# Key norms and sine products on GpSimd, query norms inside the score pass, in a two-layer hybrid attention kernel

## The chip, the cores and the metric

One core of one Trainium2 chip. The metric is the device time of one launch, in microseconds (us). Three runs of the kernel before gave 1128.81, 1129.51 and 1130.82 us; their median is 1129.51 us.

## The reference, cut to what matters

Two layers, each a SwiGLU block, an attention mixer and a second SwiGLU block, on 256 tokens of width 1024. The mixer has three branches, a (4 query heads, 2 key heads, window 128), b (4 heads through latents) and c (8 query heads, compressed, selected and windowed keys). The change touches these lines of it:

```
def rms_norm(x, g):
    y = xf * lax.rsqrt(jnp.mean(xf * xf, axis=-1, keepdims=True) + EPS)
    return (y * g).astype(x.dtype)
def apply_rope(x, cos, sin):
    return concatenate([x1 * c - x2 * s, x2 * c + x1 * s])

qa = apply_rope(rms_norm(heads(a_q, A_HEADS), a_qk_g[0]), cos64, sin64)
ka = apply_rope(rms_norm(heads(a_k, A_KV_HEADS), a_qk_g[1]), cos64, sin64)
qc = rms_norm(heads(c_q, C_HEADS), c_qk_g[0])
qc_rot = apply_rope(qc, cos64, sin64)
k_cmp = rms_norm(compress_blocks(heads(c_kc, C_KV_HEADS), ...), c_qk_g[1])
s = jnp.einsum('bqhgd,bjhd->bhgqj', qc, k_cmp).astype(jnp.float32) * scale   # then masked softmax over 15 keys
```

A query's norm is one number per token and head, so it can be applied to the query or to the query's row of scores. The scale is 64 ** -0.5 for a and c and 96 ** -0.5 for b.

## The kernel before, in words

There is no planner: the order of the work is written out by hand, one program for each engine, and semaphores tie them. `PREP` names the steps that VectorE (DVE) finishes in the mixer, in order: lat, qb, kb, qa, kc, cq, cr, ck, cmp. `AUX` names small results that TensorE (PE) puts into four PSUM banks in turn (`aux_open` waits until the one four places before has been copied out), with the engine that copies each out. SyncE issues the large weight loads; GpSimd (POOL) builds the rotary tables at the start and is idle after that. `link` marks an instruction whose result the next one on the same engine waits for.

The mixer's weights are projected in five chunks. The last two, F_CQ (c's queries) and F_CK (c's selected and windowed keys and values), are projected in split precision: for each of four quarters q, ScalarE (ACT) rounds the rows into `mwh` (`round_rows`, L1327), DVE forms the remainder `mwl` (`rest_rows`, L1915), and PE multiplies (`project_split`, L861, L862, and L866, which is the part that reads `mwl`). `copy_proj` (L1286, L1287) on ACT squares and copies a finished chunk to SBUF.

DVE's part (`mixer` in the vector program), in its order: norm of a's queries and keys (`heads_rstd`, `by_rstd`), remainders of F_CQ's quarters 0 and 1, rotation of a's heads (step qa), remainders of quarters 2 and 3; then the compressed keys, `kcn`, 15 partitions by 2 heads of 64: square, sum, inverse root in eight small instructions (`rsqrt`, L1488 to L1495), product with the root, with the gain, twice, into `kcd` (step kc); remainders of F_CK's quarters 0 to 2; the norm of c's queries in place (step cq); the remainder of F_CK's quarter 3; the rotation of c's queries (`rope`: one product with the cosines L1537, two halves with the sines L1538 and L1539, one sum L1549; step cr).

PE's part: `project_split(F_CQ)`, turns of qa, ka (`doubled`) and kc, `scores(l, 0)`, `project_split(F_CK)`, then a loop over n from 1: `scores(n)`, for n = 1 the turns of c's normed queries cq0 and cq1, then `values(n - 2)`, `turn_probs(n - 1)`, for n = 1 the compressed scores (L1063), and from n = 4 on the output projection `mix_out` (L723, L725, L727), which first waits for `cmpT`.

The 12 units n are pairs of heads: 0 and 1 of a, 2 and 3 of b, 4 to 11 of c, selected and windowed in turn. For each head, `rescore` on DVE (L1980 for 128 columns, L1982 for 256) reads the scores from PSUM, multiplies them by `-scale`, adds the mask and takes the row's minimum; ACT takes the exponentials (`exponents`); `normalise` on DVE multiplies by the reciprocal of the sum. Between units 1 and 4 DVE also does `key_norms` and `key_ropes` for the selected and windowed keys, `compressed_scores` (L2020 to L2024) and `compressed_probs`:

```
                    V.tensor_tensor_reduce(e[:, 0:P], ps[:, i, 0:P], cst[:, C_CAUSAL:C_CAUSAL + P], -scale, least,
                                           ALU.add, ALU.min, st[:, 2:3])
```

`least` is a per-partition value from memory (`nsink`) for branch a and the number 3e38 for the others; `-scale` is a number for all.

Of the kernel before, what the change touches and what calls it, by code (L numbers as in the profile page):

```python
# [33 lines left out]
I32 = mybir.dt.int32  # L34
ALU = mybir.AluOpType
# [75 lines left out]
def hybrid_kernel(nc, x, c, positions, ada_w, ada_b, norm_g, ffn_w_in, ffn_w_out, w_in, w_out,  # L111
                  a_sinks, a_qk_g, b_q_lat_g, b_kv_lat_g, b_w_uq, b_w_ukv, b_qk_nope_g, b_qk_rope_g,
                  c_qk_g, c_cmp_pe, c_cmp_w1, c_cmp_w2, c_gate_w, c_gate_b, consts, out):
    with ExitStack() as ctx:
        def sb(name, shape, dt=F32):
            return ctx.enter_context(nc.sbuf_tensor(name, shape, dt))

        def sem(name):
            return ctx.enter_context(nc.semaphore(name))
# [117 lines left out]
        def ET(n, i):  # L237
# [6 lines left out]
        csc = fa[:, :, 0:C_H * NCMP].rearrange("p a (h b) -> p a h b", h=C_H)  # L244
        trg = cqT[:, 0:3, :].rearrange("p a n -> p (a n)")
        kwt = sb("kwt", [P, SEQ])
        cst16 = sb("cst16", [P, 3, NT * C_H])


# [132 lines left out]
        def head(n, i):  # L382

            br, hh = UNITS[n][0], 2 * UNITS[n][1] + i
            half = slice(64 * i, 64 * i + 64)
            if br == "a":
                return (qaT[half, hh // 2, :], kaT[half, hh // 2, :],
                        lambda t: pa[:, t, 384 + hh // 2 * HD:384 + hh // 2 * HD + HD], cst[:, C_BAND:C_CAUSAL + P], SC64)
            if br == "b":
                return qbT[:, hh, :], kbT[:, hh, :], lambda t: kvb[:, t, hh, HD:P], mlate[:, :], SC96  # L390
            win = int(br == "win")
            kv = hh // 4
            off = 256 + 128 * win + kv * HD
            return (crT[half, hh // 2, :], ckT[half, 2 * win + kv, :],
                    lambda t: pk[:, t, off:off + HD], mlate[:, :], SC64)

        def head_at(l, n, i):

# [208 lines left out]
        def _(pe):  # L607
# [337 lines left out]
            def mixer(l):  # L945
# [83 lines left out]
                cq = pq[:, :, :].rearrange("p t (a n) -> p t a n", a=C_H)  # L1029

                for n in range(1, NU + 3):
                    if n < NU:
                        if n == 4:
# [1 line left out]
                            pe.wait_ge(*aux_done("kw", l))  # L1035
                        scores(l, n)
                    if n == 1:
                        pe.wait_ge(prep, prep_at(l, "cq"))
                        pairs("cq0", cq, (0, 1))
                        pairs("cq1", cq, (2, 3))  # L1040
# [78 lines left out]
        def _(act):  # L1119
# [177 lines left out]
            def mixer(l):  # L1297
# [54 lines left out]
                for q in range(3):  # L1352
# [5 lines left out]
                nc.scalar.copy(kcT[:, :, 0:NCMP], ps[:, aux_bank("kc"), 0:2 * P].rearrange("p (g b) -> p g b", g=2)  # L1358
                               [:, :, 0:NCMP]).then_inc(aux_act, 1)

                round_rows(F_CK, 3)

                def exponents(n, i):
# [19 lines left out]
                    exponents(0, i)  # L1383
                copy_proj(l, 4)
                for n in range(1, NU + 1):
                    if n == 1:
                        out_of(l, "cq0", cqT[:, 0:2, :])
                        out_of(l, "cq1", cqT[:, 2:4, :])
                    if n == 2:
                        out_of(l, "cr0", crT[:, 0:2, :])  # L1390
                        out_of(l, "cr1", crT[:, 2:4, :])
                    for i in range(2):
                        if n < 3 and i == 0:
                            turned_probs(n - 1, 0)
# [27 lines left out]
        def _(pool):  # L1422
# [46 lines left out]
                i = V.tensor_copy(cs[:, 1, :, hf:2 * hf], tv[:, 1, :, lo:lo + hf])  # L1469
            i.then_inc(tables, 1)  # L1470


        @block.vector
        def _(dve):
# [7 lines left out]
                ins.then_inc(chain_s, 1)  # L1482
                dve.wait_ge(chain_s, chain["n"])

            def rsqrt(n, p=P):

                s, t, r = ssb[0:p, 0:n], newt[0:p, 0:n], rst[0:p, 0:n]
                link(ts(r.bitcast(I32), s.bitcast(I32), -0.5, float(0x5F3759DF), ALU.mult, ALU.add))  # L1488
                link(tt(t, r, r, ALU.mult))
                link(stt(t, t, -0.1875, s, ALU.mult, ALU.mult))  # L1490
                link(stt(r, t, 0.5625, r, ALU.add, ALU.mult))
                link(tt(t, r, r, ALU.mult))
                link(stt(t, t, 64.0 / 9.0, s, ALU.mult, ALU.mult))
                link(stt(t, t, 10.0 / 3.0, t, ALU.subtract, ALU.mult))
                link(stt(r, t, 5.0, r, ALU.add, ALU.mult))  # L1495

            def heads_rstd(src, dim, tmp=None):

                p, a, n, d = src.shape
                if tmp is None:  # L1500
# [328 lines left out]
            def mixer(l):  # L1829
# [121 lines left out]
                spread = lambda ap, n=C_H: ap.rearrange("p (t b) -> p t b", t=NT).unsqueeze(2)\  # L1951
# [19 lines left out]
                def rescore(n, i):  # L1971
# [44 lines left out]
                def compressed_scores():  # L2016
# [94 lines left out]
```

## Time and profile before

| | us |
|---|---|
| median of the runs | 1129.51 |
| the profiled execution, its own time | 1130.08 |
| its span, first to last instruction | 1128.3 |
| PE busy | 1084.1 (96%) |
| DVE busy | 831.3 (74%) |
| ACT busy | 499.5 (44%) |
| POOL busy | 12.0 (1%), all before 22.2 us |

The mixers stand at 220 to 380 us (layer 0) and 766 to 926 us (layer 1) of the span. The numbers below are of layer 0; layer 1 repeats them 546.2 us later. "us" in a row is a time from the start of the span, then a duration. In a timeline "[2.72 <-ACT mwh L1327]" means that the engine had been idle for 2.72 us, and what ended it. The granted clock of TensorE is given as a share of its full speed.

### The profile page before, as it was taken

What the parts mean: (1) busy time and instruction counts of PE and PEld (TensorE: products, weight loads), DVE (VectorE), ACT (ScalarE), POOL (GpSimd) and SP (SyncE); (2) the same over time, 40 slices, a digit from 0 to 9 for tenths busy, and PEclk for the clock granted to TensorE, in tenths of its full rate; (3) what the DMA queues carried; (4) which work ended last, traced back from release to release, by engine and by line L of the source; (5) the groups of instructions that cost most, each with busy time, mean ns of one, the idle gap of its engine ahead of it and who ended that gap; (6) DMA issues with size and microseconds to landing.
All of it is one profiled execution on the core that took longest, in us unless ns stands there. A gap on an engine that the chain in (4) does not pass through costs nothing.

```text
span 1128.3 us, 13797 instructions
## 1 busy us (share of the span) xinstructions
PE 1084.1 (96%) x5221; PEld 837.4 (74%) x5221; DVE 831.3 (74%) x1502; ACT 499.5 (44%) x868; POOL 12.0 (1%) x30
## 2 busy tenths in 40 slices
PE   5999999999989999999999999999998999999998
PEld 1688888865766588888878888886576667888887
DVE  1766997886988785876687789886879787655644
ACT  2543342324567563343534433422255566433431
POOL 4000000000000000000000000000000000000000
PEclk9999999999989999999999999999998999999999
DMA  9799999454612179896439999954582113876631
GB/s 360 259 378 363 372 378 326 148 180 129 224 62 76 38 252 330 305 325 209 162 113 334 342 387 384 355 194 156 115 294 80 53 61 115 269 250 230 199 112 74
DMA packets 149366, 253.70 MB, mean 225 GB/s; under 512 B 9639, under 2 KB 119861, under 8 KB 141109
## 3 DMA queue, kind: packets, MB, share of 16 engines
q1 hardware_dynamic: 148596, 251.53, 65.1%
q10 hardware_dynamic: 704, 1.30, 0.3%
q8 instruction: 41, 0.67, 0.2%
q14 instruction: 25, 0.20, 0.1%
HBM read 251.76 MB, written 1.05 MB: 224 GB/s over the span
## 4 chain that ended last, share of the span: by engine, by line
PE 84%; DVE 11%; ACT 2%; issue 1%; DMA 1%; SPq 0%; DVEq 0%; ACTq 0%
PE ps L693 12%; PE ps L695 12%; PE ps L694 12%; PE ps L723 8%; PE ps L727 8%; PE ps L725 8%; PE ps L845 6%; DVE mwl L1915 2%; PE ps L705 2%; PE ps L674 1%; PE ps L672 1%; PE ps L673 1%; PE ps L901 1%; DMA wide<-in_ada_w_dram 1%; PE ps L890 1%
## 5 line engine op out<-in xcount | busy, mean ns | idle before, releaser
L693 PE MATMUL ps<-wh,uh 128*128 128x512 f32 x576 | 227.2, 395 | 0.0
L695 PE MATMUL ps<-wlo,uh 128*128 128x512 f32 x576 | 224.5, 390 | 0.0
L694 PE MATMUL ps<-wh,ul 128*128 128x512 f32 x576 | 224.3, 389 | 0.0
L1645 DVE TENSOR_TENSOR wlo<-wide,wh 128x1024 fp32r<-128x1024 f32 x176 | 207.6, 1220 | 15.7 <-ACT wh L1183 13.9
L1183 ACT CAST wh<-wide 128x1024 fp32r<-128x1024 f32 x176 | 175.9, 1049 | 16.7 <-DMA wide<-in_ffn_w_in_dram 16.7
L1255 ACT ACTIVATE fs<-ps 128x512 f32<-128x512 f32 x40 | 24.0, 599 | 282.3 <-PE ps L695 273.1
L1800 DVE TENSOR_TENSOR fa<-fs,ps 128x512 f32<-128x512 f32 x40 | 27.5, 688 | 137.8 <-ACT fs L1255 137.2
L723 PE MATMUL ps<-th,fh 128*128 128x512 f32 x320 | 128.1, 400 | 0.0
L695 PEld LDWEIGHTS ps<-wlo,uh 128*128 128x128 f32 x576 | 108.1, 188 | 23.0
L727 PE MATMUL ps<-tlo,fh 128*128 128x512 f32 x320 | 125.0, 390 | 0.0
L725 PE MATMUL ps<-th,fl 128*128 128x512 f32 x320 | 124.6, 390 | 0.0
L694 PEld LDWEIGHTS ps<-wh,ul 128*128 128x128 f32 x576 | 108.3, 188 | 21.6
L693 PEld LDWEIGHTS ps<-wh,uh 128*128 128x128 f32 x576 | 108.2, 188 | 21.4
L1673 DVE TENSOR_TENSOR tlo<-tall,th 128x1024 fp32r<-128x1024 f32 x104 | 123.4, 1219 | 0.0
L1656 DVE SCALAR_TENSOR_TENSOR acc<-ada,cond,acc 128x2048 f32<-128x2048 f32 (+1 forms) x49 | 100.2, 2044 | 22.9 <-DMA ada<-in_ada_w_dram 22.5
L1190 ACT CAST th<-tall 128x1024 fp32r<-128x1024 f32 x104 | 105.2, 1051 | 10.8 <-DMA tall<-in_ffn_w_out_dram 10.8
L725 PEld LDWEIGHTS ps<-th,fl 128*128 128x128 f32 x320 | 60.2, 188 | 12.7 <-issue 1.0
L727 PEld LDWEIGHTS ps<-tlo,fh 128*128 128x128 f32 x320 | 60.0, 188 | 12.8
L723 PEld LDWEIGHTS ps<-th,fh 128*128 128x128 f32 x320 | 60.1, 188 | 12.6 <-issue 1.0
L845 PE MATMUL ps<-wide,u 128*128 128x416 f32 (+2 forms) x192 | 68.6, 515 | 0.3
L845 PEld LDWEIGHTS ps<-wide,u 128*128 128x128 f32 x192 | 36.0, 190 | 29.5 <-issue 23.6
L1195 ACT CAST fh<-ps 128x512 fp32r<-128x512 f32 x40 | 23.5, 587 | 60.3 <-PE ps L705 60.3
(363 smaller groups left out, 1548.2 us busy)
## 6 DMA issues: line engine op xcount, KB each, us to landing
wide<-in_ffn_w_in_dram SPq DMA_DIRECT2D x176, 512.0 KB, 6.6
ada<-in_ada_w_dram SPq DMA_DIRECT2D x60, 1024.0 KB, 7.1
tall<-in_ffn_w_out_dram SPq DMA_DIRECT2D x44, 1024.0 KB, 5.2
wide<-in_w_in_dram SPq DMA_DIRECT2D x14, 1024.0 KB, 7.5
tall<-in_w_out_dram SPq DMA_DIRECT2D x8, 1024.0 KB, 8.6
ada<-in_ada_w_dram SPq DMA_DIRECT2D x16, 512.0 KB, 5.9
wide<-in_c_cmp_w_dram SPq DMA_DIRECT2D x4, 1024.0 KB, 10.1
wide<-in_w_in_dram SPq DMA_DIRECT2D x4, 832.0 KB, 7.9
```

What stands on the lines that cost most here:

```text
L693: mm(o, uh[:, k, rows_], wh[:, hsl, :, k, :], start=(k == 0), stop=False, skip_group_check=True)
L694: mm(o, ul[:, k, rows_], wh[:, hsl, :, k, :], start=False, stop=False, skip_group_check=True)
L695: i = mm(o, uh[:, k, rows_], wlo[:, s, :, k, :], start=False, stop=(k == KD - 1), skip_group_check=True)
L723: mm(y[:, t, hf, :], hi[:, toks], th[:, slot, a, cols], start=(first and x == 0), stop=False, skip_group_check=True)
L725: mm(y[:, t, hf, :], lo[:, toks], th[:, slot, a, cols], start=False, stop=False, skip_group_check=True)
L727: i = mm(y[:, t, hf, :], hi[:, toks], tlo[:, slot, a, cols], start=False, stop=(last and x == len(rows) - 1), skip_group_check=True)
L845: i = mm(ps[:, banks + t, 0:width], u[:, k, t * P:(t + 1) * P], wv[:, k, :], start=(k == 0), stop=(k == KD - 1))
L1183: nc.scalar.copy(wh[:, (n + 1) % 2, :, 2 * c:2 * c + 2, :], raw).then_inc(wh_ready, 1)
L1190: nc.scalar.copy(th[:, n % 2, m % 2, :], tall[:, n % 2, m % 2 * DM:(m % 2 + 1) * DM]).then_inc(th_ready, 1)
L1645: tt(wlo[:, n % 2, :, ks, :], raw, wh[:, (n + 1) % 2, :, ks, :].bitcast(F32), ALU.subtract)\
L1656: stt(part, piece, cond[:, k:k + 1], part, ALU.mult, ALU.add).then_inc(ada_used, 1)
L1673: tt(tlo[:, n % 2, m % 2, :], tall[:, n % 2, m % 2 * DM:(m % 2 + 1) * DM], th[:, n % 2, m % 2, :].bitcast(F32), ALU.subtract).then_inc(tl_ ...
```

## The change

- GpSimd gets `key_norm(l)`: it waits for the copy-out of "w2" (ACT) and for step lat, then norms the compressed keys with 23 instructions: 17 products or sums of two tensors and 6 with constants, each linked to the next except the first of the last two. It increments `kc_normed`, for which PE's turn of kc now waits. DVE's block for it goes; steps kc and cq go from `PREP`.
- GpSimd gets `sine_halves(l)`: after the copy of c's query projection and step qa, the two sine products of c's rotation into `T2` (512 elements per partition each). DVE does the cosine product, waits for `sines`, and adds.
- c's queries are no longer multiplied by their root (L1945). `score_root` puts the negated root, with the 1/8 of the scale in it, into `qroot`, and for branch a into `aroot`; `rescore` takes its multiplier from there, a column of memory per token block, in place of the number. Branch b keeps a number. Of a's six heads DVE now multiplies only the two key heads by their root, and a's key table has a factor -8.
- The compressed scores are multiplied by the roots in one added DVE instruction of 240 elements; the maximum becomes a minimum, and the exponential's scale -1. Their buffer `csc` moves from `fa` to `ada`.
- PE's turns of cq0 and cq1, now of unnormed queries, move from n = 1 to between the turn of kc and `scores(l, 0)`, behind a wait for the copy of the projection; ACT's copies of them move before its rounding of F_CK's quarter 3.
- The rotary tables with gain (`gained`) are made by an instruction with a constant factor in place of a plain product.

```diff
-        PREP = ["lat", "qb", "kb", "qa", "kc", "cq", "cr", "ck", "cmp"]
+        PREP = ["lat", "qb", "kb", "qa", "cr", "ck", "cmp"]
...
-                pe.wait_ge(prep, prep_at(l, "kc"))
+                pe.wait_ge(kc_normed, l + 1)
                 turn(l, "kc", [(P * g, kcd[:, g, :, :].rearrange("p a n -> p (a n)")) for g in range(2)])
+                pe.wait_ge(pcopy, l * 10 + 8)
+                cq = pq[:, :, :].rearrange("p t (a n) -> p t a n", a=C_H)
+                pairs("cq0", cq, (0, 1))
+                pairs("cq1", cq, (2, 3))
                 pe.wait_ge(*aux_done("ka", l))
                 pe.wait_ge(pcopy, l * 10 + 6)
                 scores(l, 0)
...
+                out_of(l, "cq0", cqT[:, 0:2, :])
+                out_of(l, "cq1", cqT[:, 2:4, :])
                 round_rows(F_CK, 3)
...
+            def key_norm(l):
+                pool.wait_ge(*aux_done("w2", l))
+                pool.wait_ge(prep, prep_at(l, "lat"))
+                kc, tmp = kcn[0:NCMP, :, :], kcd[0:NCMP, :, 0, :]
+                s, t, r = (cst16[0:NCMP, x, 0:2] for x in range(3))
+                link(tt(tmp, kc, kc, ALU.mult))
+                w = HD // 2
+                while w > 1:
+                    link(tt(tmp[:, :, 0:w], tmp[:, :, 0:w], tmp[:, :, w:2 * w], ALU.add))
+                    w //= 2
...
+            def sine_halves(l):
+                pool.wait_ge(pcopy, l * 2 * len(CHUNKS) + 2 * 4)
+                pool.wait_ge(prep, prep_at(l, "qa"))
+                tt(t2[:, :, :, 0:hf], cq[:, :, :, hf:HD], wide_(cs[:, :, 0:hf]), ALU.mult)
+                tt(t2[:, :, :, hf:HD], cq[:, :, :, 0:hf], wide_(cs[:, :, hf:HD]), ALU.mult).then_inc(sines, 1)
...
-                dve.wait_ge(*aux_done("w2", l))
-                kc = kcn[0:NCMP, :, :].unsqueeze(2)
-                heads_rstd(kc, HD)
-                by_rstd(kc, kc)
-                for dup in range(2):
-                    i = gain(kc, G_C + HD, kcd[0:NCMP, :, dup, :].unsqueeze(2))
-                i.then_inc(prep, 1)
-                dve.wait_ge(prep, prep_at(l, "kc"))
...
-                heads_rstd(cq, HD, v4(cq2[:, :, :], C_H))
-                r = rst[:, 0:NT * C_H].rearrange("p (a n) -> p a n", a=NT).unsqueeze(3).broadcast_to([P, NT, C_H, HD])
-                tt(cq, cq, r, ALU.mult).then_inc(prep, 1)
-                dve.wait_ge(prep, prep_at(l, "cq"))
+                roots = score_root(qroot, v4(cq2[:, :, :], C_H))
                 rest_rows(F_CK, 3)
-                rope(cq, cs_of(T_CQ), [qr[:, :, :, :]]).then_inc(prep, 1)
+                t1, t2 = (ap[:, :].rearrange("p (a n d) -> p a n d", a=NT, n=C_H) for ap in (T1, T2))
+                link(tt(t1, cq, cs_of(T_CQ)[:, 0, :, :].unsqueeze(2).broadcast_to([P, NT, C_H, HD]), ALU.mult))
+                dve.wait_ge(sines, l + 1)
+                tt(qr[:, :, :, :], t1, t2, ALU.add).then_inc(prep, 1)
...
-                    V.tensor_tensor_reduce(e[:, 0:P], ps[:, i, 0:P], cst[:, C_CAUSAL:C_CAUSAL + P], -scale, least,
+                    V.tensor_tensor_reduce(e[:, 0:P], ps[:, i, 0:P], cst[:, C_CAUSAL:C_CAUSAL + P], scale[0], least,
...
-                    link(V.tensor_reduce(over(0), csc, AX.X, ALU.max))
+                    link(tt(csc, csc, roots.unsqueeze(3).broadcast_to([P, NT, C_H, NCMP]), ALU.mult))
+                    link(V.tensor_reduce(over(0), csc, AX.X, ALU.min))
```

## Rows read from the trace of the kernel before

**Rows 1.** Timeline of DVE, layer 0's mixer: start, duration, engine, line, operation, forms, [idle].
```profile
281.49 2.36 DVE L1915 TENSOR_TENSOR mwl<-wide,mwh 128x1024 fp32r<-128x1024 f32 x2 [2.72 <-ACT mwh L1327]
...
287.54 2.36 DVE L1915 TENSOR_TENSOR mwl<-wide,mwh 128x1024 fp32r<-128x1024 f32 x2
...
292.42 0.48 DVE L1516 TENSOR_TENSOR kcd<-kcn,gn 15x128 f32<-15x128 f32 x2
...
296.35 1.21 DVE L1503 TENSOR_REDUCE ssb<-cq 128x16 f32<-128x1024 f32 x1
...
299.48 1.23 DVE L1945 TENSOR_TENSOR acc<-acc,rst 128x1024 f32<-128x1024 f32 x1
...
303.02 0.69 DVE L1538 TENSOR_TENSOR sq<-acc,fa 128x512 f32<-128x512 f32 x1
...
305.81 0.35 DVE L1980 CUSTOM_DVE_ANT_0 acc<-ps,cst,nsink 128x128 f32<-128x128 f32 x1
...
309.74 0.34 DVE L1980 CUSTOM_DVE_ANT_0 early<-ps,cst,nsink 128x128 f32<-128x128 f32 x1
...
318.99 0.29 DVE L1980 CUSTOM_DVE_ANT_0 acc<-ps,cst 128x128 f32<-128x128 f32 x1
...
321.05 0.41 DVE L2024 TENSOR_TENSOR fa<-fa,cst 128x240 f32<-128x240 f32 x1
```

**Rows 2.** Timeline of PE, the same mixer.
```profile
288.91 1.10 PE L866 MATMUL ps<-mwl,muh 128*128 128x512 f32 x4
...
293.46 0.38 PE L878 MATMUL ps<-cst,kcd 128*128 128x128 f32 x2
295.41 0.93 PE L890 MATMUL ps<-kaT,qaT 64*128 64x128 f32 x8 [1.57 <-ACT kaT L1295]
296.27 0.50 PE L861 MATMUL ps<-mwh,muh 128*128 128x512 f32 x1
...
307.38 0.93 PE L890 MATMUL ps<-kaT,qaT 64*128 64x128 f32 x8
...
332.25 0.47 PE L723 MATMUL ps<-th,uh 128*128 128x512 f32 x1 [2.20 <-ACT cmpT L1295]
```

**Rows 3.** Timeline of ACT, the same mixer.
```profile
282.36 0.25 ACT L1349 COPY vrep<-ps 128x128 f32<-128x128 f32 x1
...
293.78 0.60 ACT L1287 COPY acc<-ps 128x512 f32<-128x512 f32 x1
...
309.75 0.57 ACT L1279 COPY acc<-ps 128x512 f32<-128x512 f32 x1
...
364.98 0.40 ACT L1370 ACTIVATE sq<-sq,stat 128x128 f32<-128x128 f32 x1 [0.70 <-DVE stat L1982]
```

**Rows 4.** Windows: stretch, then length and busy (count) per engine, PEclk, DMA share, GB/s.
```profile
330.00:340.00 10.00, 7.80 (x39) 5.84 (x39) 6.62 (x31) 5.42 (x18) 0.00 (x0) 0.83 0.00 0
340.00:350.00 10.00, 10.00 (x65) 6.95 (x65) 7.84 (x35) 6.88 (x22) 0.00 (x0) 1.00 0.33 106
```

**Rows 5.** Timeline of POOL at the start of the kernel.
```profile
8.70 0.35 POOL L1447 TENSOR_TENSOR cqT<-cst,posf 128x96 f32<-128x96 f32 x1
...
13.79 0.59 POOL L1456 TENSOR_TENSOR cqT<-cqT 128x192 f32<-128x192 f32 x1
14.47 0.69 POOL L1455 TENSOR_SCALAR cqT<-cqT 128x192 f32<-128x192 f32 x1
```

**Rows 6.** Timeline of DVE at the start of the kernel.
```profile
12.27 0.16 DVE L1583 SCALAR_TENSOR_TENSOR rst<-newt,rst 128x1 f32<-128x1 f32 x1
...
13.92 0.48 DVE L1583 SCALAR_TENSOR_TENSOR rst<-newt,rst 128x1 f32<-128x1 f32 x1
...
14.74 0.16 DVE L1585 SCALAR_TENSOR_TENSOR newt<-newt 128x1 f32<-128x1 f32 x1
```

**Rows 7.** Chain of work that ended last, two steps of the output projection.
```profile
333.25 0.43 PE ps L723
...
339.99 0.23 PE ps L723
```

More of the change, by code:

```diff
@@ L243, in hybrid_kernel @@
         cp = fs[:, :, :].rearrange("p a (h b) -> p a h b", h=C_H)
-        csc = fa[:, :, 0:C_H * NCMP].rearrange("p a (h b) -> p a h b", h=C_H)
+        csc = ada[:, 0, 0:NT * C_H * NCMP].rearrange("p (a h b) -> p a h b", a=NT, h=C_H)
         trg = cqT[:, 0:3, :].rearrange("p a n -> p (a n)")
         kwt = sb("kwt", [P, SEQ])
+        aroot, qroot = sb("aroot", [P, NT * 6]), sb("qroot", [P, NT * C_H])
         cst16 = sb("cst16", [P, 3, NT * C_H])
@@ L282, in hybrid_kernel @@
         chain_s = sem("chain")
+        kc_normed, sines = sem("kc_normed"), sem("sines")
         muh_ready, mul_ready_, mwh_ready, mwl_ready, mwh_used = (
@@ L387, in head @@
                 return (qaT[half, hh // 2, :], kaT[half, hh // 2, :],
-                        lambda t: pa[:, t, 384 + hh // 2 * HD:384 + hh // 2 * HD + HD], cst[:, C_BAND:C_CAUSAL + P], SC64)
+                        lambda t: pa[:, t, 384 + hh // 2 * HD:384 + hh // 2 * HD + HD], cst[:, C_BAND:C_CAUSAL + P],
+                        [aroot[:, 6 * t + hh:6 * t + hh + 1] for t in range(NT)])
             if br == "b":
-                return qbT[:, hh, :], kbT[:, hh, :], lambda t: kvb[:, t, hh, HD:P], mlate[:, :], SC96
+                return qbT[:, hh, :], kbT[:, hh, :], lambda t: kvb[:, t, hh, HD:P], mlate[:, :], [-SC96, -SC96]
             win = int(br == "win")
@@ L394, in head @@
             return (crT[half, hh // 2, :], ckT[half, 2 * win + kv, :],
-                    lambda t: pk[:, t, off:off + HD], mlate[:, :], SC64)
+                    lambda t: pk[:, t, off:off + HD], mlate[:, :],
+                    [qroot[:, C_H * t + hh:C_H * t + hh + 1] for t in range(NT)])
         def head_at(l, n, i):
@@ L1037, in mixer @@
                     if n == 1:
-                        pe.wait_ge(prep, prep_at(l, "cq"))
-                        pairs("cq0", cq, (0, 1))
-                        pairs("cq1", cq, (2, 3))
                         pe.wait_ge(pcopy, l * 10 + 10)
@@ L1385, in mixer @@
                 for n in range(1, NU + 1):
-                    if n == 1:
-                        out_of(l, "cq0", cqT[:, 0:2, :])
-                        out_of(l, "cq1", cqT[:, 2:4, :])
                     if n == 2:
@@ L1400, in mixer @@
                             act.wait_ge(cmp_shift, l + 1)
-                            A(csc, csc, ACT.Exp, scale=SC64).then_inc(cmp_exp, 1)
+                            A(csc, csc, ACT.Exp, scale=-1.0).then_inc(cmp_exp, 1)
                         if n == 4 and i == 0:
@@ L1470, in _ @@
             i.then_inc(tables, 1)
+            def key_norm(l):
[8 more added lines that the diff above has]
+                    w //= 2
+                link(tt(s.unsqueeze(2), tmp[:, :, 0:1], tmp[:, :, 1:2], ALU.add))
+                link(ts(s, s, 1.0 / HD, EPS, ALU.mult, ALU.add))
+                link(ts(r.bitcast(I32), s.bitcast(I32), -0.5, float(0x5F3759DF), ALU.mult, ALU.add))
+                v = cst16[0:NCMP, 2, 2:4]
+                link(tt(t, r, r, ALU.mult))
+                link(tt(t, t, s, ALU.mult))
+                link(ts(t, t, -0.1875, 0.5625, ALU.mult, ALU.add))
+                link(tt(r, t, r, ALU.mult))
+                link(tt(t, r, r, ALU.mult))
+                link(tt(t, t, s, ALU.mult))
+                link(ts(t, t, 64.0 / 9.0, None, ALU.mult))
+                link(ts(v, t, -10.0 / 3.0, None, ALU.add))
+                link(tt(t, t, v, ALU.mult))
+                link(ts(t, t, 5.0, None, ALU.add))
+                link(tt(r, t, r, ALU.mult))
+                link(tt(kc, kc, r.unsqueeze(2).broadcast_to([NCMP, 2, HD]), ALU.mult))
+                g = gn[0:NCMP, G_C + HD:G_C + 2 * HD].unsqueeze(1).broadcast_to([NCMP, 2, HD])
+                for dup in range(2):
+                    i = tt(kcd[0:NCMP, :, dup, :], kc, g, ALU.mult)
+                i.then_inc(kc_normed, 1)
+                pool.wait_ge(kc_normed, l + 1)
@@ new lines, in sine_halves @@
+            def sine_halves(l):
+                hf, cs = HD // 2, fa[:, 0, :].rearrange("p (e t n) -> p e t n", e=2, t=NT)[:, 1, :, :]
+                cq = pq.rearrange("p t (n d) -> p t n d", n=C_H)
+                t2 = T2.rearrange("p (a n d) -> p a n d", a=NT, n=C_H)
+                wide_ = lambda ap: ap.unsqueeze(2).broadcast_to([P, NT, C_H, hf])
+                pool.wait_ge(pcopy, l * 2 * len(CHUNKS) + 2 * 4)
+                pool.wait_ge(prep, prep_at(l, "qa"))
+                tt(t2[:, :, :, 0:hf], cq[:, :, :, hf:HD], wide_(cs[:, :, 0:hf]), ALU.mult)
+                tt(t2[:, :, :, hf:HD], cq[:, :, :, 0:hf], wide_(cs[:, :, hf:HD]), ALU.mult).then_inc(sines, 1)
@@ L1473, in _ @@
+            for l in range(DEPTH):
+                key_norm(l)
+                sine_halves(l)
         @block.vector
@@ L1483, in link, with rsqrt @@
                 dve.wait_ge(chain_s, chain["n"])
-            def rsqrt(n, p=P):
-                s, t, r = ssb[0:p, 0:n], newt[0:p, 0:n], rst[0:p, 0:n]
-                link(ts(r.bitcast(I32), s.bitcast(I32), -0.5, float(0x5F3759DF), ALU.mult, ALU.add))
+            def rsqrt(n, p=P, root=None):
+                s, t, r = ssb[0:p, 0:n], newt[0:p, 0:n], rst[0:p, 0:n] if root is None else root
+                seed = float(0x5F3759DF) if root is None else float(0x5F3759DF - 2 ** 31)
+                link(ts(r.bitcast(I32), s.bitcast(I32), -0.5, seed, ALU.mult, ALU.add))
                 link(tt(t, r, r, ALU.mult))
@@ L1505, in heads_rstd, with score_root @@
                 rsqrt(a * n, p)
+            def score_root(root, sums):
+                p, a, n, d = sums.shape
+                link(V.tensor_reduce(ssb[:, 0:a * n].rearrange("p (a n) -> p a n", a=a), sums, AX.X, ALU.add))
+                link(ts(ssb[:, 0:a * n], ssb[:, 0:a * n], HD * EPS, None, ALU.add))
+                rsqrt(a * n, root=root[:, :])
+                return root[:, :].rearrange("p (a n) -> p a n", a=a)
             def by_rstd(src, dst):
@@ L1524, in gained @@
             def gained(lo, a):
-                hf, c = HD // 2, cs_of(a)
+                hf, c, by = HD // 2, cs_of(a), -8.0 if a == T_AK else 1.0
                 g = lambda x, y: gn[:, lo + x:lo + y].unsqueeze(1).broadcast_to([P, NT, y - x])
-                tt(c[:, 0, :, :], cs64[:, 0, :, :], g(0, HD), ALU.mult)
-                tt(c[:, 1, :, 0:hf], cs64[:, 1, :, 0:hf], g(hf, HD), ALU.mult)
-                return tt(c[:, 1, :, hf:HD], cs64[:, 1, :, hf:HD], g(0, hf), ALU.mult)
+                stt(c[:, 0, :, :], cs64[:, 0, :, :], by, g(0, HD), ALU.mult, ALU.mult)
+                stt(c[:, 1, :, 0:hf], cs64[:, 1, :, 0:hf], by, g(hf, HD), ALU.mult, ALU.mult)
+                return stt(c[:, 1, :, hf:HD], cs64[:, 1, :, hf:HD], by, g(0, hf), ALU.mult, ALU.mult)
             def turned_halves(src, cs, t1, t2):
@@ L1919, in mixer @@
                 qk = v4(pa[:, :, 0:384], 6)
-                heads_rstd(qk, HD, v4(qk2[:, :, :], 6))
-                by_rstd(qk, qk)
+                root = score_root(aroot, v4(qk2[:, :, :], 6))[:, :, A_H:6].unsqueeze(3).broadcast_to([P, NT, A_KV, HD])
+                link(tt(qk[:, :, A_H:6, :], qk[:, :, A_H:6, :], root, ALU.mult))
                 for q in range(2):
@@ L1979, in rescore @@
                         dve.wait_ge(pt_ready, head_at(l, n - 2, i))
-                    V.tensor_tensor_reduce(e[:, 0:P], ps[:, i, 0:P], cst[:, C_CAUSAL:C_CAUSAL + P], -scale, least,
+                    V.tensor_tensor_reduce(e[:, 0:P], ps[:, i, 0:P], cst[:, C_CAUSAL:C_CAUSAL + P], scale[0], least,
                                            ALU.add, ALU.min, st[:, 2:3])
-                    V.tensor_tensor_reduce(e[:, P:3 * P], ps[:, i, P:3 * P], head(n, i)[3], -scale, least,
+                    V.tensor_tensor_reduce(e[:, P:3 * P], ps[:, i, P:3 * P], head(n, i)[3], scale[1], least,
                                            ALU.add, ALU.min, st[:, 3:4]).then_inc(nm_ready, 1)
```

1 line of the change is left out of this document (removed).

## The prediction, made before the change was run

> **What bounds the kernel now.** I read the timelines of DVE, PE and ACT over layer 0's mixer side by side, then the windows; layer 1 repeats them. Three stretches matter.
>
> First, 281.5 to 307.4 us: PE multiplies F_CQ and F_CK almost without a gap. Quarter 2's part that reads `mwl` starts at 288.91 [rows 2], and DVE's pair of remainders for quarters 2 and 3 runs from 287.54 for 2.36 us [rows 1], so quarter 2's is ready at about 288.7: PE has 0.2 us to spare there. The turn of kc starts at 293.46; then PE is idle 1.57 us until ACT has copied `kaT`, does `scores(0)` at 295.41, starts F_CK at 296.27 and `scores(1)` at 307.38 [rows 2].
>
> Second, 306 to 332 us: DVE is the bound. Its scan of unit 1 starts at 309.74 [rows 1], although `scores(1)` began at 307.38 and takes 0.93 us [rows 2], so the scores were there at 308.3. DVE is 1.44 us late, and from there it works without a pause up to the scan of unit 4. PE waits for the result of that, 2.20 us, until `cmpT` at 332.25 [rows 2].
>
> Third, 336 to 380 us: PE is the bound, busy 10.00 of 10 us with DVE at 7.84 [rows 4].
>
> So work taken from DVE before 309.74 is worth 1.44 us per mixer and no more, for behind DVE stands PE's projection of F_CK, which the change does not shorten. Work added to DVE after 309.74 counts in full until 332. Work added on PE's way before 307.4 counts where it exceeds those 1.44 us.
>
> **Part by part (us, per mixer).**
>
> *Key norm off DVE.* DVE's block lies between the remainders' end (287.54 + 2.36 = 289.90) and 292.42 + 0.48 = 292.90 [rows 1]: 3.0 go. The remainders of F_CK then end at about 293.5, and DVE waits for the copy of the projection, 293.78 + 0.60 = 294.38 [rows 3], where the reduction for the roots can start instead of at 296.35 [rows 1]: 2.0 are left.
>
> *Query product and sine halves off DVE.* The product is 1.23, the halves two of 0.69 which overlap to 1.2 [rows 1]. DVE would be ready for the first scan at 305.81 - 2.0 - 1.2 - 1.2 = 301.4. All that counts of these 4.4 is the 1.44, as unit 1's scan must wait for PE.
>
> *A's query product* falls away where DVE idles 2.72 us for `mwh` [rows 1]: nothing. That idle time hides it; were it gone, 0.7 would count. *Tables with gain*: an operation of the same size, under PE's earlier projections; nothing, between -0.3 and +0.3.
>
> *Root column as the multiplier.* The scan of 128 columns takes 0.35 and 0.34 with one operand from memory (`nsink`) and 0.29 with none [rows 1]: 0.06 per instruction. I take it to add up for the second column of branch a. Unit 1 has four such instructions, +0.24; the first head of unit 4, on which the end of the DVE stretch hangs, two, +0.12. The other units of c have 0.24 each under PE. At the end of the mixer ACT waits for such a scan (0.70 at 364.98 [rows 3]); that may cost between 0 and 0.2, I take 0.
>
> *Roots on the compressed scores.* One more instruction of 240 elements: 0.41 [rows 1] and a link, +0.44, in full.
>
> *Turns of cq0 and cq1.* They go into PE's gap before 295.41: the projection's copy ends at 294.38, eight turns take about 0.9 (half of the 0.38 that two take, as they overlap), and `kaT` is there at 295.4. I take 0, between 0 and +0.3. They leave n = 1, which is under DVE; nothing. ACT's two copies before F_CK's quarter 3 have 8 us until PE needs it.
>
> *Key norm on GpSimd.* It can start at 282.61 (end of ACT's L1349 [rows 3]). A product of 96 elements takes 0.35 there and one of 192 takes 0.59 [rows 5], that is 0.11 + 0.0025 per element; one with a constant on 192 takes 0.69 [rows 5], some 0.2 on two elements; from 0.59 at 13.79 to the next start at 14.47 a link costs 0.09. Seventeen products: four of 128 elements at 0.43, one each of 64, 32, 16, 8 and 4 at 0.27, 0.19, 0.15, 0.13 and 0.12, eight of two at 0.12; with six of 0.21 and the links 6.9 in all, done at 289.5. PE wants the result at 293.46. Undisturbed, the move has 4 us of cover.
>
> *The same beside DVE.* What the trace shows of two-tensor work on both engines at once: DVE's L1583 takes 0.16 at 12.27, and 0.48 at 13.92, where GpSimd's product ran from 13.79 to 14.38; it ended at 14.40, with it [rows 6, 5]. L1585 at 14.74, inside GpSimd's constant product (14.47 to 15.16), took its 0.16 [rows 6, 5]. So GpSimd's two-tensor products hold up DVE's two-tensor instructions, its constant ones don't. The opposite direction has no row, and from 282.6 to 293.5 DVE does nothing but two-tensor instructions: remainders of 1.18 and the rotation.
>
> The Trainium skill ("SBUF — State Buffer", section "Who interferes with whom") says that a VectorE instruction with two SBUF inputs and a GpSimd instruction that reads SBUF exclude each other, and that whichever comes second is held until the first has ended. The row at 13.92 agrees with it; the row at 14.74 does not, since there GpSimd read SBUF with one input and VectorE was not held. By that rule in both directions the sum would be the +5.4 below, and without it the -1.3.
>
> Bounds: (a) nothing is held: 0. (b) DVE alone is held. Between its remainders of quarters 1 and 2 stand nine rotation instructions, and GpSimd's first seven products fall among them: 0.43 + 0.27 + 0.19 + 0.15 + 0.13 + 0.12 + 0.12 = 1.41. Quarter 2's remainder comes at 290.1, PE wanted it at 288.91: PE is 1.2 late from there. (c) Both are held, in turn. Then GpSimd gets one product per DVE instruction; one more passes in the rotation and nine are left. Five pass with the five remainders, 5 x 1.3, until 295.4; the last four, three of them of 128 elements, need 2.1: done at 297.5. PE, at the turn of kc at 294.7, waits 2.8. Behind that wait stand the turns of kc, cq0, cq1 and `scores(0)` (0.4 + 0.9 + 0.9), then F_CK: it starts at 299.6 instead of 296.27, +3.3.
>
> *Sine products.* 512 elements at 0.0025 + 0.11 are 1.4 each, from 294.4 to 297.2, and DVE wants them at 300. Holding DVE's small steps costs 1.5 of the 6 us that it has until 308.3. Nothing.
>
> **The sum.** With DVE out of the way, the stretch after `scores(1)` starts 1.44 early and has 0.24 + 0.44 + 0.12 = 0.80 more work. Per mixer: (a) -1.44 + 0.80 = -0.64; (b) -0.64 + 1.2 = +0.6; (c) -0.64 + 3.3 = +2.7. For two mixers -1.3, +1.1 and +5.4. The row at 13.92 speaks for (b) at least; whether a DVE instruction holds GpSimd is open, but a resource that one of two engines waits for is likely one that both wait for. I take the middle of (b) and (c), +3.3: the profiled execution's 1130.08 becomes 1133.4, and the median, 0.57 under it, 1129.51 + 3.3 = 1132.8.
>
> **Rivals.**
> 1. *No interference.* GpSimd is done by 290, PE never waits, -1.3: 1128.2. For it: the key norm occupies 15 partitions only, its products are short, and L1583 is a single row. Against it: that row's end, to 0.02 us. This is the case on the other side; it decides as soon as `kc_normed` comes before 294 and quarter 2's remainder before 288.9.
> 2. *The slow stretch of PE goes too.* After its 2.20 us of waiting, PE runs at a granted clock of 0.83 in the mean of 330 to 340 [rows 4]: steps of 0.43 where the same take 0.23 at full clock (2.4 GHz against the lower level's 1.2) [rows 7]; twelve of them stand in that state, 2.4 us. If in case (a) another spacing keeps the clock up in both mixers: 1128.2 - 4.8 = 1123.4; in one, 1125.8. Against it: the wait before it, for DVE, stays as long.
> 3. *The scans become the bound after 336.* Eight units of c at 0.24 are 1.9 per mixer. All of it on the path on top of (a): -1.3 + 3.8 = +2.5, 1132.0. Against it: DVE has 2.2 of 10 us free [rows 4].
> 4. *The sines come late.* GpSimd starts them only after the key norm. In case (c) that is 297.5, done at 300.3, still before 308.3 + 3.3. Only at double the price would it count: +1 per mixer over (c).
>
> **How the numbers follow.** Interference 0.50, rival 1 0.27, rival 2 0.11, rival 3 0.07, rival 4 or something else that is late 0.05. A change of 0.2% (2.3 us) is what can be told from none here. Interference puts 0.40 above that and 0.10 within; rival 1 0.20 within and 0.07 below, by a part of rival 2's gain; rival 2 below; rival 3 above; the last 0.03 above, 0.02 within. So faster 0.18, same 0.32, slower 0.50. The forecast's own range is 1130.6 to 1135.0; the range over cases 1127.0 to 1136.0, which leaves out rival 2 and the far end of rival 4.
>
> **What would show it.** Interference: GpSimd's first products at several times 0.43 and 0.27, ending with DVE's remainders; DVE's rotation longer than before by 1.4; a wait of PE at quarter 2 and at the turn of kc. Right without it: key norm done in 7 us. In either case scans at 0.35 in c, a start of unit 1's scan 0.9 after `scores(1)`, a DVE stretch 0.8 longer up to `cmpT`. The prediction is wrong if PE starts F_CK within 0.5 of its old distance from 281.5.

## The result: 7.8 us slower

The changed kernel took 1137.49 us (median of 4 runs, 1136.35 to 1139.64) against 1129.71 us for the kernel before (median of 4, the extra run included): 1.0070 times the time, 95% interval 1.0057 to 1.0082. The direction was the forecast's, the size more than twice its 3.3 us, and above the upper end of its own range, 1135.0, and of the range over cases, 1136.0.

The profiled execution took 1136.35 us, its span 1134.5. From the page of the changed kernel, busy time by engine:

```profile
span 1134.5 us, 13819 instructions
...
PE 1086.5 (96%) x5221; PEld 837.6 (74%) x5221; DVE 831.8 (73%) x1470; ACT 500.4 (44%) x868; POOL 42.0 (4%) x80
```

DVE is as busy as before (831.3) although it has 32 instructions fewer: what it gave away it pays back in instructions that are longer. GpSimd's busy time rose by 30 us.

Timeline of GpSimd in layer 0's mixer, after:

```profile
281.91 1.41 POOL L1480 TENSOR_TENSOR kcd<-kcn 15x128 f32<-15x128 f32 x1 [260.11 <-ACT vrep L1352]
283.40 2.57 POOL L1483 TENSOR_TENSOR kcd<-kcd 15x64 f32<-15x64 f32 x5
...
287.24 1.18 POOL L1489 TENSOR_TENSOR cst<-cst 15x2 f32<-15x2 f32 x1
288.50 1.06 POOL L1490 TENSOR_TENSOR cst<-cst 15x2 f32<-15x2 f32 x1
289.65 1.04 POOL L1491 TENSOR_SCALAR cst<-cst 15x2 f32<-15x2 f32 x1
290.77 1.05 POOL L1492 TENSOR_TENSOR cst<-cst 15x2 f32<-15x2 f32 x1
291.91 1.06 POOL L1493 TENSOR_TENSOR cst<-cst 15x2 f32<-15x2 f32 x1
293.05 0.18 POOL L1494 TENSOR_TENSOR cst<-cst 15x2 f32<-15x2 f32 x1
...
294.49 0.18 POOL L1499 TENSOR_TENSOR cst<-cst 15x2 f32<-15x2 f32 x1
...
295.22 0.86 POOL L1503 TENSOR_TENSOR kcd<-kcn,gn 15x128 f32<-15x128 f32 x2
296.15 1.30 POOL L1515 TENSOR_TENSOR sq<-acc,fa 128x512 f32<-128x512 f32 x1
297.42 1.26 POOL L1516 TENSOR_TENSOR sq<-acc,fa 128x512 f32<-128x512 f32 x1
```

Five instructions on two elements take 1.04 to 1.18 us; the sixth, of the same size, takes 0.18. DVE over the same time:

```profile
282.99 0.89 DVE L1596 TENSOR_TENSOR sq<-acc,fs 128x512 f32<-128x512 f32 x1
...
287.15 5.77 DVE L1974 TENSOR_TENSOR mwl<-wide,mwh 128x1024 fp32r<-128x1024 f32 x5
294.04 1.22 DVE L1561 TENSOR_REDUCE ssb<-cq 128x16 f32<-128x1024 f32 x1 [1.12 <-ACT acc L1290]
295.29 0.40 DVE L1562 TENSOR_SCALAR ssb<-ssb 128x16 f32<-128x16 f32 x1
295.73 0.38 DVE L1539 TENSOR_SCALAR qroot<-ssb 128x16 int32<-128x16 int32 x1
...
296.35 1.14 DVE L1541 SCALAR_TENSOR_TENSOR newt<-newt,ssb 128x16 f32<-128x16 f32 x1
297.52 1.20 DVE L1542 SCALAR_TENSOR_TENSOR qroot<-newt,qroot 128x16 f32<-128x16 f32 x1
298.75 0.17 DVE L1543 TENSOR_TENSOR newt<-qroot 128x16 f32<-128x16 f32 x1
```

DVE's five remainders run from 287.15 to 292.92, 1.15 apiece, as fast as before [rows 1]. One small GpSimd instruction falls to each; when DVE stops at 292.9 they cost 0.18 again, and still do beside DVE's reduction (294.49, inside L1561). When the small ones are DVE's (L1541, L1542, 0.17 each with the sine products back on DVE, run e2 below) and the long ones GpSimd's sine products, DVE waits. DVE's one-input instructions L1562 and L1539 are not free of it either: 0.40 and 0.38 beside GpSimd's L1503, 0.17 each in the kernel before.

PE in the same mixer (compare [rows 2]), and the windows around its restart:

```profile
288.43 1.19 PE L870 MATMUL ps<-mwl,muh 128*128 128x512 f32 x4
...
296.13 0.44 PE L882 MATMUL ps<-cst,kcd 128*128 128x128 f32 x2 [2.88 <-POOL kcd L1503]
296.40 1.09 PE L882 MATMUL ps<-cst,acc 128*128 128x128 f32 x8
297.42 1.65 PE L894 MATMUL ps<-kaT,qaT 64*128 64x128 f32 x8
299.00 0.79 PE L865 MATMUL ps<-mwh,muh 128*128 128x512 f32 x1
...
310.87 0.93 PE L894 MATMUL ps<-kaT,qaT 64*128 64x128 f32 x8
...
335.13 0.76 PE L727 MATMUL ps<-th,uh 128*128 128x512 f32 x1 [2.32 <-ACT cmpT L1298]
```

```profile
293.00:297.00 4.00, 1.12 (x11) 0.88 (x10) 2.82 (x5) 2.17 (x6) 3.29 (x10) 1.00 0.85 272
297.00:301.00 4.00, 4.00 (x18) 2.77 (x16) 3.79 (x8) 3.54 (x5) 1.68 (x2) 0.57 0.76 252
301.00:305.00 4.00, 4.00 (x19) 3.30 (x18) 3.90 (x10) 0.64 (x4) 0.00 (x0) 1.00 0.00 0
```

I count from DVE's first remainder of F_CQ, 281.49 before [rows 1] and, in the changed kernel's timeline, 280.71 after. F_CK starts at 14.8 before and 18.3 after (+3.5). That is not all waiting: `scores(0)` runs at the lower clock level, 1.65 us instead of 0.93 [rows 2], so some 0.7 of the 3.5 is the clock's. `scores(1)` comes at 25.9 and 30.2 (+4.3, the extra 0.8 is again the clock, granted at 0.57 from 297 to 301); unit 1's scan at 28.3 and 31.1 (+2.9); the output projection at 50.8 and 54.4 (+3.7). The mixer as a whole, from PE's first matmul of F_CQ to the first residual sum, takes 102.7 us in both layers instead of 99.1, two times 3.6 or 7.2 us. The medians differ by 7.8; the spans of the two profiled executions differ by 6.2 (1134.5 and 1128.3), so outside the mixers this one execution was 1.0 shorter than the one before.

Scans with a column from memory, first one of unit 0 and one of unit 1:

```profile
303.44 0.41 DVE L2030 CUSTOM_DVE_ANT_0 acc<-ps,cst,nsink 128x128 f32<-128x128 f32 x1
...
311.83 0.41 DVE L2030 CUSTOM_DVE_ANT_0 early<-ps,cst,nsink 128x128 f32<-128x128 f32 x1 [4.25 <-PE ps L894]
```

### The profile page after: what moved, and what is told of

Its sections match the earlier page's. It is cut to its first block, busy times and chain, and to the rows that moved or that the text cites. A ratio compares the mean times of both kernels' runs of the same rounds, so it can differ in the third digit from the quotient of the medians.

```text
span 1134.5 us, 13819 instructions
## 1 busy us (share of the span) xinstructions
PE 1086.5 (96%) x5221; PEld 837.6 (74%) x5221; DVE 831.8 (73%) x1470; ACT 500.4 (44%) x868; POOL 42.0 (4%) x80
## 3 DMA queue, kind: packets, MB, share of 16 engines
HBM read 251.76 MB, written 1.05 MB: 223 GB/s over the span
## 4 chain that ended last, share of the span: by engine, by line
PE 84%; DVE 7%; POOL 2%; ACT 2%; DMA 2%; issue 2%; SPq 0%; DVEq 0%; POOLq 0%; ACTq 0%
PE ps L699 12%; PE ps L697 12%; PE ps L698 12%; PE ps L727 8%; PE ps L731 7%; PE ps L729 7%; PE ps L849 6%; DMA ada<-in_ada_w_dram 2%; PE ps L709 2%; PE ps L894 1%; PE ps L678 1%; PE ps L676 1%; PE ps L677 1%; PE ps L905 1%; PE ps L663 1%
```

## The experiments

All were timed in five rounds against the kernel before, whose median was 1129.89 in the first four, 1129.47 in the next four and 1129.56 in the last. Each is the changed kernel with an edit, but for e6 and e11. The ratios are not the quotients of the medians; where the two differ by much, as in e6, both are read. "The mixer" is the stretch defined above, in the run's profiled execution.

**e1, the key norm on DVE.**

```diff
-                key_norm(l)            # GpSimd
...
+                dve.wait_ge(*aux_done("w2", l))
+                kc = kcn[0:NCMP, :, :].unsqueeze(2)
+                heads_rstd(kc, HD)
+                by_rstd(kc, kc)
...
+                i.then_inc(kc_normed, 1)
```

> The changed kernel with the compressed keys' norm given back to DVE, at its old place; GpSimd keeps the sine products, everything else of the change stays. Theory (GpSimd's key norm holds up PE's turn of kc): the 2.9 us wait of PE before the turn of kc goes, PE starts F_CK some 14.8 us after F_CQ instead of 18.3, and the time falls by about 4.3 us per mixer, to 1128.0 to 1129.5. Rival A (the root columns and the added product on the compressed scores cost more than thought): still 3 us or more over the kernel before, 1132 or more. Rival B (the sine products are the cause): stays near 1137.

1129.99 us, ratio 0.9997 (0.9989 to 1.0006), 0.5 above the expected range. The whole loss is gone. In its profiled execution each mixer takes 98.7 us, unit 1's scan comes 26.9 after PE's first matmul of F_CQ (28.2 before) and the output projection 23.28 after that scan (22.51 before). Rivals A and B fall.

**e2, the sine products on DVE.**

```diff
-                sine_halves(l)         # GpSimd
...
+                rope(cq, cs_of(T_CQ), [qr[:, :, :, :]]).then_inc(prep, 1)
```

> The changed kernel with the two sine products given back to DVE; GpSimd keeps the key norm. Theory: PE's wait for the key norm stays at 2.9 us, DVE is ready for unit 0 some 1 us later but still waits for PE before unit 1: within 1 us of the changed kernel, 1136.5 to 1138.5. Rival B (the sine products hold DVE's inverse root up, 1.14 and 1.20 us for two instructions, and that is the loss): 3 us or more below the changed kernel.

1138.05 us, ratio 1.0071 (1.0059 to 1.0083), that of the changed kernel (1.0070). L1541 and L1542 of the changed kernel take 0.17 each here instead of 1.14 and 1.20, and PE's wait is 2.85: the 2 us for which the inverse root was held up lie under PE's work.

**e3, PE asks later.** The turn of kc stands behind `scores(1)`.

```diff
-                pe.wait_ge(kc_normed, l + 1)
-                turn(l, "kc", ...)
                 pe.wait_ge(pcopy, l * 10 + 8)
...
                     if n == 1:
+                        pe.wait_ge(kc_normed, l + 1)
+                        turn(l, "kc", ...)
                         pe.wait_ge(pcopy, l * 10 + 10)
```

> The changed kernel, but PE turns kc, and ACT copies it, only after scores(1) and before the compressed scores; cq0 and cq1 come before it. GpSimd does the same work as in the changed kernel. Theory: the key norm is done at about 296 us, PE asks for it at 308, no wait is left, DVE's first remainders are still held a few tenths: 4 us per mixer less than the changed kernel, 1128.0 to 1130.0. Rival C (what GpSimd does to DVE costs by itself, wait or not): 1132 or more. Rival A as before: 1132 or more.

1130.25 us, ratio 1.0009 (0.9999 to 1.0020), 0.25 above the expected range. GpSimd's chain takes as long as in the changed kernel (14.2 us), and nobody waits for it: the loss is PE's wait, and not, in the main, what GpSimd does to DVE. That has a small price: in the profile F_CK still starts 0.4 us later than before, and unit 1's scan comes 27.2 after PE's first matmul of F_CQ where e1 has 26.9. Rivals A and C fall. The twelve runs lie wide, 1127.84 to 1136.46 us, and the profiled one was the slowest: its mixers take 101.5 us, with a granted clock of 0.68 and 0.66 over 320 to 330 and 330 to 340 us where e1 has 1.00 and 0.83. Whether its faster runs had these stretches at full clock, no trace shows.

**e4, a number as the multiplier** (the query norms are left out of the scores of a and c).

```diff
-                        [aroot[:, 6 * t + hh:6 * t + hh + 1] for t in range(NT)])
+                        [-SC64, -SC64])
```

> The changed kernel with the fixed scale in place of the root columns in the score pass of branches a and c; this leaves the query norms out of those scores. Theory: 0.06 us less for each scan with a column, 0.36 us per mixer of them on the path (unit 1 and the first head of unit 4), at most 0.2 more at the end: 0.7 to 1.2 us below the changed kernel, 1136.3 to 1136.8. Rival A: the scans are the bound in the units of c, 2 us per mixer: 1133.5 or less. GpSimd's instructions and PE's wait are the same in both.

1136.45 us, ratio 1.0059 (1.0046 to 1.0072); by the ratios 0.11% or 1.2 us below the changed kernel, though the two intervals overlap. In the profiled execution the mixers take 102.4, 0.35 less each, as forecast for the columns on the path (0.36). The columns are not the bound under PE.

**e5, DVE idle while GpSimd works.**

```diff
+                dve.wait_ge(kc_normed, l + 1)
                 for q in range(3):
                     rest_rows(F_CK, q)
```

> The changed kernel with one wait added on DVE: it begins F_CK's remainders of quarters 0 to 2 only when GpSimd's key norm is done. Theory (each small GpSimd instruction from 287 us on took 1.05 us because a DVE remainder of 1.15 us ran and held it): with DVE idle after quarter 3 of F_CQ, at about 289.4, the rest of the key norm goes at 0.2 us apiece, is done 2.5 to 3 us earlier, PE's wait before the turn of kc falls from 2.9 to under 0.7 us, and the time to 1129.5 to 1131.5. Rival D (these are GpSimd's own prices in a linked chain): the chain is as long as before, PE's wait 2.9 us, the time 1137 or more.

1134.26 us, ratio 1.0043 (1.0026 to 1.0060): a miss, 2.8 us above the expected range. On whether GpSimd's instructions are held, the rows decide. Timelines of e5, GpSimd and then DVE and PE:

```profile
289.06 1.06 POOL L1490 TENSOR_TENSOR cst<-cst 15x2 f32<-15x2 f32 x1
290.21 0.18 POOL L1491 TENSOR_SCALAR cst<-cst 15x2 f32<-15x2 f32 x1
290.47 0.18 POOL L1492 TENSOR_TENSOR cst<-cst 15x2 f32<-15x2 f32 x1
290.74 0.18 POOL L1493 TENSOR_TENSOR cst<-cst 15x2 f32<-15x2 f32 x1
...
294.68 1.75 POOL L1515 TENSOR_TENSOR sq<-acc,fa 128x512 f32<-128x512 f32 x1 [0.64 <-POOL kcd L1503]
296.39 2.27 POOL L1516 TENSOR_TENSOR sq<-acc,fa 128x512 f32<-128x512 f32 x1
```

```profile
294.07 5.67 DVE L1974 TENSOR_TENSOR mwl<-wide,mwh 128x1024 fp32r<-128x1024 f32 x3 [4.00 <-POOL kcd L1503]
299.67 1.21 DVE L1561 TENSOR_REDUCE ssb<-cq 128x16 f32<-128x1024 f32 x1
```

```profile
294.10 0.44 PE L882 MATMUL ps<-cst,kcd 128*128 128x128 f32 x2 [0.31 <-POOL kcd L1503]
```

The same three instructions (L1491 to L1493) that took 1.04 to 1.06 take 0.18 with DVE idle, and PE's wait falls from 2.88 to 0.31. Rival D falls. What the expectation missed: DVE's three remainders start only at 294.07, fall among the sine products and take 5.67; in the kernel before they fit between 292.9 and the reduction at 296.35 [rows 1]. So DVE is late for unit 0, and PE waits 0.67 for its scan before `scores(1)`. In layer 1 the three take 4.57 and PE has no such wait; the mixers take 102.2 and 100.1.

**e6, the sine products alone**, in the kernel before, after step cq.

```diff
+                pool.wait_ge(prep, prep_at(l, "cq"))
+                tt(t2[:, :, :, 0:hf], ...)      # and the other half
...
-                rope(cq, cs_of(T_CQ), [qr[:, :, :, :]]).then_inc(prep, 1)
+                link(tt(t1, cq, ..., ALU.mult))
+                dve.wait_ge(sines, l + 1)
+                tt(qr[:, :, :, :], t1, t2, ALU.add).then_inc(prep, 1)
```

> The kernel before with one part of the change: the two sine products of c's rotation on GpSimd, here after the query norm (step cq), so beside DVE's remainder of F_CK's quarter 3 and its cosine product. Theory of mutual holding: the four two-tensor instructions of the two engines go one after the other, 1.2 + 1.3 + 1.2 + 1.3, then the sum; DVE is ready for unit 0 1.0 to 1.5 us later than before, 1131.5 to 1133. Naive sum (DVE loses 1.2 us): 1127 to 1128.

1133.08 us in the median of 12, ratio 1.0021 (1.0009 to 1.0033). The median is 3.6 us over the kernel before, the ratio says 2.4; the runs spread from 1128.31 to 1134.27, so the size is uncertain, but it is no gain. Timelines of e6, GpSimd, DVE and PE:

```profile
301.29 2.33 POOL L1480 TENSOR_TENSOR sq<-acc,fa 128x512 f32<-128x512 f32 x1 [279.46 <-DVE acc L1959]
303.57 2.29 POOL L1481 TENSOR_TENSOR sq<-acc,fa 128x512 f32<-128x512 f32 x1
```

```profile
301.23 1.23 DVE L1929 TENSOR_TENSOR mwl<-wide,mwh 128x1024 fp32r<-128x1024 f32 x1
302.38 2.32 DVE L1963 TENSOR_TENSOR sq<-acc,fa 128x1024 f32<-128x1024 f32 x1
305.96 1.23 DVE L1965 TENSOR_TENSOR qr<-sq 128x1024 f32<-128x1024 f32 x1 [1.26 <-POOL sq L1481]
```

```profile
308.92 0.93 PE L891 MATMUL ps<-kaT,qaT 64*128 64x128 f32 x8 [0.99 <-DVE stat L1999]
```

Remainder, first half, cosine product, second half: one after the other from 301.2 to 305.9, 4.7 us until the sum. DVE alone needs 3.6 for the same, 300.74 to 304.35 in the kernel before, as a half costs it 0.6 and GpSimd over 1.1. So the move makes DVE 1.1 us later, its scan of unit 0 is late, and PE waits 0.99 for it before `scores(1)`.

**e7, PE kept busy during its wait.**

```diff
+                pe.wait_ge(pcopy, l * 10 + 6)
+                keep_warm(12)
                 pe.wait_ge(kc_normed, l + 1)
```

> The changed kernel with 12 idle multiplications of 512 columns (2.7 us at full clock) on PE in front of its wait for kc_normed. Theory (0.7 us of the loss per mixer is PE at the lower clock level just after the wait, in scores(0) and the first five matmuls of F_CK): the wait's place is filled, F_CK runs at full clock from its start, 0.5 to 0.9 us per mixer less, 1135.5 to 1136.5. If the clock is no part of it: within 0.5 us of 1137.5.

1135.04 us, ratio 1.0048 (1.0036 to 1.0060): 2.4 us under the changed kernel, a little more than expected. `kcd` comes as late, but `scores(0)` takes 0.93 again, F_CK's matmuls follow each other at 0.23 from the second on, and each mixer takes 101.4 us. F_CK starts 17.5 after PE's first matmul of F_CQ (+2.7 over the kernel before instead of +3.5) and `scores(1)` at 28.6 (+2.8 instead of +4.3). So 1.2 to 1.5 us per mixer of the loss is the lower clock level after the wait.

**e8, the gates' arithmetic before unit 1**, with e1's edit, and branch a's queries normed as before.

```diff
+                dve.wait_ge(gate_exp, l + 1)
+                link(ts(gt[:, :, :], gt[:, :, :], 1.0, None, ALU.add))
+                link(V.reciprocal(gt[:, :, :], gt[:, :, :]))
```

> The changed kernel with the key norm on DVE again, and two more edits that take work out of DVE's stretch after unit 1's scan: the gates' sum and reciprocal (0.65 us) done right after c's rotation, where DVE waits for PE, and branch a's queries normed as in the kernel before, with a number as the multiplier (0.24 us at unit 1). Theory (DVE is idle before unit 1 and the bound from there to cmpT): per mixer 0.9 us less than the version with the keys on DVE, 1127.6 to 1128.6, under the kernel before. If that stretch were not DVE's: as that version, 1129.5 to 1130.5.

1128.26 us, ratio 0.9986 (0.9977 to 0.9994): as expected, and 0.14% faster than the kernel before.

**e9, e8 without any GpSimd work in the mixer** (the diffs of e2 and e8 together).

> The version with the gates early (e8), and the sine products back on DVE too: nothing of the mixer is left on GpSimd. In e8 unit 1's scan came 27.5 us after the start of F_CQ, 0.6 later than PE allows, with DVE as the bound. Theory: the sine products add 1.2 us to DVE there and give back 1.0 us of what they held in F_CK's remainders (4.57 us for three in e8, 3.50 before); DVE is the bound, 0 to 0.8 us per mixer more than e8: 1128.3 to 1129.8. If the sine products on GpSimd were worth their full 1.2 us per mixer: 1130.5 or more.

1128.10 us, ratio 0.9982 (0.9972 to 0.9991): as e8, and 0.2 under the expected range. The sine products on GpSimd are worth nothing that can be measured.

**e10, e11, e12: PE kept busy before the output projection**, in e8, in the kernel before and in e9.

```diff
+                    if n == 4:
+                        keep_warm(10, 4)
                     for k in range(KD):
                         if n in MIX_AT[k]:
```

> e8 with 10 idle multiplications of 512 columns on PE in its wait of 2.3 us for cmpT, before the output projection. Theory (the forecast's rival 2: after that wait PE runs a dozen matmuls at the lower clock level, 0.43 us a step where 0.23 is the price at full clock): the slow stretch goes or is halved, 1.0 to 2.4 us per mixer less: 1123.5 to 1126.5. If the clock falls all the same: 1128 to 1129.

> The kernel before with the same 10 idle multiplications in front of the output projection. Theory as for e10: 2 to 4.8 us less than the kernel before, 1124.7 to 1127.5. If the wait is not what lowers the clock: 1129.3 to 1130.

> e9 and the idle multiplications together: the difference to e9 is that of e10 to e8, 2 to 4.8 us, 1124 to 1127.5.

1126.10 (0.9961, 0.9948 to 0.9974), 1127.19 (0.9970, 0.9958 to 0.9982) and 1126.15 us (0.9961, 0.9949 to 0.9973): 2.0 to 2.4 us less by the medians in each pair. Timeline of PE in e11, where [rows 2] has the idle 2.20 us, and its window:

```profile
329.11 2.32 PE L613 MATMUL ps<-zb 128*128 128x512 bf16 x10
331.46 0.47 PE L723 MATMUL ps<-th,uh 128*128 128x512 f32 x1
331.77 0.40 PE L725 MATMUL ps<-th,ol 128*128 128x512 f32 x1
```

```profile
330.00:340.00 10.00, 9.96 (x58) 6.93 (x56) 8.04 (x33) 6.30 (x21) 0.00 (x0) 1.00 0.00 0
```

The clock stands at 1.00 where it was 0.83 [rows 4]. The first twelve matmuls of the output projection start within 2.6 us instead of 4.2, and each mixer takes 97.5 us instead of 99.1.

## Why the direction was right and the size wrong

*What bounds the kernel.* Right. In e1, where PE waits for nothing new, unit 1's scan comes 1.3 us earlier in the mixer (1.44 forecast), and no more, though DVE gave up two and a half.

*Work added after unit 1's scan.* Right: 23.30 us from that scan to the output projection in the changed kernel instead of 22.51 [rows 1, 2], +0.79; forecast 0.80. The scan of a takes 0.41 with two columns, 0.35 with one and 0.29 with none [rows 1].

*The key norm on GpSimd: the term that was mis-sized.* The forecast had three bounds and took the middle of (b) and (c), +1.65 per mixer. Measured is +3.6, beyond (c), +2.7. The mechanism of (c), in turn, one GpSimd instruction per remainder, is what the trace shows and e5 confirms. The start of F_CK moved by 3.5 us and (c) said 3.3, but that nearness is partly luck: with the clock held up (e7) it moved by 2.7, so (c) was 0.6 too high and the clock, which it did not have, added 0.8. Averaging with (b), a case in which only DVE is held, was the mistake: DVE in fact lost least, 0.4 us at quarter 2's remainder instead of 1.41, and by e3 its share comes to 0.3 to 0.4 us per mixer.

*The premise that GpSimd's constant instructions pass freely* was drawn from L1585 at 14.74 [rows 6]. It failed in the other direction: L1491, with one tensor read, took 1.04 beside DVE's remainder and 0.18 without.

The rule of the Trainium skill ("SBUF — State Buffer", section "Who interferes with whom"), that a two-input VectorE instruction and a GpSimd instruction that reads SBUF exclude each other and the second one waits, held in both directions: 1.05 against 0.18 on GpSimd, 1.14 and 1.20 against 0.17 on DVE, and for L1491 as well. The row that the forecast set against it stays unexplained. So does the hold of L1562 and L1539, which have one input each (0.40 and 0.38 against 0.17).

*The missing term: PE's clock after the new wait.* The forecast gave the lower level a place only as a gain (rival 2). The wait of 2.9 us brought it on from `scores(0)` to the first matmuls of F_CK; e7 sizes it at 1.2 us per mixer by the time and 1.5 by the start of `scores(1)`. So +3.6 is made of the late start of F_CK without the clock, +2.7, the clock, +1.5, the 1.4 by which unit 1's scan follows `scores(1)` sooner (0.96 us instead of 2.36), and +0.8 of added work.

*Sine products: nothing.* Right in the changed kernel (e2), and e9 shows nothing gained by them either. Put beside two long DVE instructions, as in e6, they cost.

*Rivals.* Rival 1, no interference, is out; its sum is near what e3 and e1 give without the wait (forecast 1128.2, measured 1130.25 and 1129.99). That the forecast's -1.3 did not come out there is not explained: e1's mixers are 0.4 us shorter each in the profile, its median is not. Rival 2's mechanism is real, but the forecast sized it too high: of the twelve matmuls after the wait, in the kernel before, some eight stand at 0.43 us a step, the first three and the last do not, so that the stretch costs 1.6 us per mixer and not 2.4. e11 gets 2.4 us from the two mixers by the medians and 1.6 in each by the profile. In e8's profile the slow stretch is absent in layer 1 with no idle matmuls at all: there PE ran at a granted clock of 0.66 from 872 to 877 us, before the wait, the wait was 1.11 instead of 2.31, the twelve started within 2.6 us, and that mixer was 1.6 shorter than layer 0's. Rival 3 is out by e4. Rival 4 did not occur.

Open: why DVE lost so little in the rotation while GpSimd was held by each long remainder; nothing here varied the order in which the two ask.

## What to carry to other kernels

Moving small vector work to GpSimd pays only where DVE is idle or in a reduction at that time (0.18 us for two elements in both cases here): beside a row of long two-tensor DVE instructions, each linked GpSimd instruction cost a whole one of them, 1.04 to 1.18 us for two elements. Look for who waits in order behind the moved result: here PE's queue, which came 3.5 us late to F_CK; asking later, with ACT's copy moved behind it too (e3), took away all but 0.4 of that. And price a new wait of PE together with the clock after it; filling it with idle matmuls gave 2.4 us both in the changed kernel and, at another wait, in the kernel before.

## What was not expected of the hardware

A GpSimd instruction on two elements takes 0.18 us alone and 1.04 to 1.18 beside DVE's two-tensor remainders. A sine product of 512 elements takes 1.26 to 1.30 beside small DVE instructions, which then wait for it, and up to 2.33 beside long ones. Four such long instructions take 4.7 us on the two engines and 3.6 on DVE alone. Ten matmuls of 512 columns in a wait of 2.2 us keep PE's granted clock at 1.00 where it fell to 0.83 in the mean of 10 us.
